# Decay scores in blocks of 32 columns, the mask ahead of a weight split, and 11 extra products ahead of the channel sums, in a two-layer HGRN2 and Mamba-2 kernel

## The reference

```python
bc = jnp.cumsum(logf, axis=2)                 # decay within a chunk
q_dec = q * jnp.exp(bc)
att = jnp.einsum('bnthd,bnshd->bnhts', q_dec, k * jnp.exp(-bc))
att = jnp.where(jnp.tril(jnp.ones((HG_CHUNK, HG_CHUNK), bool)), att, 0.0)
o_intra = jnp.einsum('bnhts,bnshv->bnthv', att, v)
...
x = x + mx[2] * rmsnorm(yx, post_norm[l, 0])
hx = modulate(rmsnorm(x, pre_norm[l, 1]), mx[3], mx[4])
```

## Time and profile before

| | |
|---|---|
| median of 3 runs | 1364.66 us (1364.53 to 1365.32) |
| the profiled execution | 1364.83 us |
| its span in the trace | 1363.1 us |
| PE busy | 1314.1 us, 96% |
| DVE busy | 873.2 us, 64% |
| ACT busy | 657.5 us, 48% |
| head loop and its tail | about 60 to 390 us |
| output projection and sums of layer 0 | about 387 to 422 us |

### The profile page before, as it was taken

The page is one execution under the profiler, slowest core; times in us unless marked ns, Lnnn a source line. Parts: engine busy times, 40 slices in busy tenths (PEclk is TensorE's granted clock), DMA queues, the critical chain, the costliest instruction groups (busy, mean ns, idle before and its releaser), DMA issues. The chain is left out here.

```text
span 1363.1 us, 21145 instructions
## 1 busy us (share of the span) xinstructions
PE 1314.1 (96%) x7954; PEld 1109.6 (81%) x7954; DVE 873.2 (64%) x1718; ACT 657.5 (48%) x1037; POOL 338.4 (25%) x236
## 2 busy tenths in 40 slices
PE   5999999999999999999999999999999999999997
PEld 2678888888775888888888867889888879899997
DVE  4577776767769544322443787877777776775673
ACT  4444444444446533323333357455555654774664
POOL 1000000000202655304553020111111140683771
PEclk9999999999999999999999999999999999999999
DMA  9633433236552443234324342633333348366753
GB/s 345 191 124 126 135 123 122 81 126 199 173 185 62 150 113 87 67 108 124 92 81 134 101 140 67 192 92 91 92 92 91 95 159 255 106 197 176 217 156 108
DMA packets 274790, 183.21 MB, mean 134 GB/s; under 512 B 6642, under 2 KB 249106, under 8 KB 274706
## 3 DMA queue, kind: packets, MB, share of 16 engines
q1 hardware_dynamic: 274162, 180.00, 44.0%
q10 hardware_dynamic: 544, 2.10, 0.4%
HBM read 181.03 MB, written 1.05 MB: 134 GB/s over the span
## 5 line engine op out<-in xcount | busy, mean ns | idle before, releaser
L2180 PE MATMUL bank<-hh,wh 128*128 128x512 f32 (+1 forms) x1298 | 457.0, 352 | 6.4 <-DVE wl L1374 4.4
L2182 PE MATMUL bank<-hh,wl 128*128 128x512 f32 (+1 forms) x1298 | 452.0, 348 | 0.0
L2181 PE MATMUL bank<-hl,wh 128*128 128x512 f32 (+1 forms) x1298 | 451.7, 348 | 0.0
L842 ACT ACTIVATE wh<-wraw 128x1024 fp32r<-128x1024 f32 (+2 forms) x265 | 257.0, 985 | 74.7 <-PE bank L2182 50.7
L2180 PEld LDWEIGHTS bank<-hh,wh 128*128 128x128 f32 x1298 | 244.5, 188 | 41.5 <-DVE wl L1374 6.6
L1374 DVE TENSOR_TENSOR wl<-wraw,wh 128x1024 fp32r<-128x1024 f32 (+2 forms) x171 | 189.3, 1127 | 138.1 <-ACT wh L842 138.0
L2182 PEld LDWEIGHTS bank<-hh,wl 128*128 128x128 f32 x1298 | 244.2, 188 | 32.5
L1835 DVE SCALAR_TENSOR_TENSOR conv<-bank,pv,conv 128x189 f32<-128x189 f32 (+3 forms) x396 | 172.4, 436 | 153.0 <-ACT conv L1113 138.0
L2181 PEld LDWEIGHTS bank<-hl,wh 128*128 128x128 f32 x1298 | 244.4, 188 | 30.2
L730 POOL TENSOR_TENSOR wl<-wraw,wh 128x1024 fp32r<-128x1024 f32 (+2 forms) x87 | 199.1, 2293 | 197.1 <-ACT wh L842 196.7
L776 POOL TENSOR_TENSOR hl<-yT,hh 128x512 fp32r<-128x512 f32 x13 | 19.6, 1535 | 368.8 <-DVE gates L1735 357.9
(11 more groups left out here) (348 smaller groups left out, 2095.6 us busy)
## 6 DMA issues: line engine op xcount, KB each, us to landing
wraw<-in_ffn_w_up SPq DMA_DIRECT2D x88, 512.0 KB, 4.0
araw<-in_ada_w SPq DMA_DIRECT2D x40, 1024.0 KB, 7.5
wraw<-in_mb_w_in SPq DMA_DIRECT2D x48, 512.0 KB, 4.0
wraw<-in_hg_w_in SPq DMA_DIRECT2D x40, 512.0 KB, 3.8
wraw<-in_ffn_w_down SPq DMA_DIRECT2D x32, 512.0 KB, 4.0
wraw<-in_mb_w_out SPq DMA_DIRECT2D x16, 512.0 KB, 4.9
gates<-in_ada_w SPq DMA_DIRECT2D x5, 1024.0 KB, 9.5
wraw<-in_hg_w_out SPq DMA_DIRECT2D x8, 512.0 KB, 4.9
```

The source lines that it names most:

```text
L842: act.activation(slot(whp, n, 0, size), wraw[:, n % SLOTS, 0:size], ACT.Copy).then_inc(w_hi, 1)
L2180: pe.matmul(dst, W, hi(k), start=(k == 0), stop=False, **skip)
L2181: pe.matmul(dst, W, lo(k), start=False, stop=False, **skip)
L2182: ins = pe.matmul(dst, L, hi(k), start=False, stop=(k == nk - 1), **skip)
```

## The change

Four edits. **Scores:** the 4 products of 128 x 128 become 16 of 32 x 32, only the diagonal blocks, going through the four groups of 32 output partitions in turn; the 8 beside the diagonal stay; the 4 of 64 x 64 become 8 of 32 x 64. Blocks that no product writes are now left from what the bank held, and DVE clears bank 6 once at the start. **Semaphore:** `qk_ready` goes up behind L1733, and a new `ke_ready` behind L1734, for which `ke` waits. **DVE:** in each turn `mask_att(p,0)` stands ahead of the split of the first weight piece. **Sums:** behind the last tile of the output projection of layer 0, 11 products go into bank 0 ahead of `both_sums`; they wait until that bank has been read and a weight piece is split.

```diff
@@ DVE, start
+        dve.memset(bank[6][:, :], 0.0)
         params(0)
@@ gate_products
-            V.tensor_tensor(parts(qx2[d]), far(C[:, :], 1 - first), w2(1 - first), ALU.mult)
-            V.tensor_tensor(ch(B), ch(A), s[:, 2, :].unsqueeze(2).to_broadcast([P, NCH, CH]), ALU.mult).then_inc(qk_ready, 1)
+            V.tensor_tensor(parts(qx2[d]), far(C[:, :], 1 - first), w2(1 - first), ALU.mult).then_inc(qk_ready, 1)
+            V.tensor_tensor(ch(B), ch(A), s[:, 2, :].unsqueeze(2).to_broadcast([P, NCH, CH]), ALU.mult).then_inc(ke_ready, 1)
@@ head loop of DVE
+            if S:
+                mask_att(p, 0)
             if h:
                 split_lo(5 * h + 3)
-            if S:
-                mask_att(p, 0)
@@ att(h, d)
-            for t in range(4):
-                r = slice(t * P, (t + 1) * P)
-                pe.matmul(bank[plan.bank(key)][:, r], gA[d][:, r], gC[d][:, r], start=True, stop=True)
+            for c in range(NCH):
+                k, r = c % 4, slice(c * CH, (c + 1) * CH)
+                pe.matmul(bank[plan.bank(key)][k * CH:(k + 1) * CH, r], gA[d][:, r], gC[d][:, r], start=True, stop=True,
+                          skip_group_check=True)
...
-                ins = pe.matmul(bank[plan.bank(key)][2 * CH * d:2 * CH * (d + 1), c:c + 2 * CH], kx2[d][:, t, :], qx2[d][:, t, :],
-                                start=True, stop=True, skip_group_check=True)
+                for j in range(2):
+                    k = 2 * d + j
+                    ins = pe.matmul(bank[plan.bank(key)][k * CH:(k + 1) * CH, c:c + 2 * CH], kx2[d][:, t, j * CH:(j + 1) * CH],
+                                    qx2[d][:, t, :], start=True, stop=True, skip_group_check=True)
@@ ke(h, d)
+            pe.wait_ge(ke_ready, 2 * h + d + 1)
@@ last_tile
+            if (l, s) == (0, 0):
+                plan.wait_emptied(pe, ("y", 0, 4))
+                stay_busy(0, 11, at["up", 0, 0, 0, 0])
```

More of the change, by code:

```diff
@@ L545, in program @@
     d_ready, small_ready, en_ready = sem("d_ready"), sem("small_ready"), sem("en_ready")
-    qk_ready, qin_ready = sem("qk_ready"), sem("qin_ready")
+    qk_ready, ke_ready, qin_ready = sem("qk_ready"), sem("ke_ready"), sem("qin_ready")
     v_ready, ket_ready, att_ready = sem("v_ready"), sem("ket_ready"), sem("att_ready")
```

## The result

The changed kernel takes **1357.03 us** (median of 4 runs, 1356.50 to 1357.08), the kernel before 1364.81 (4 runs, 1364.53 to 1365.32): ratio 0.9942, 95% interval 0.9926 to 0.9958, so 7.8 us less where 9.2 were forecast. The profiled executions took 1357.05 and 1364.83 us. The forecast stood 1.6 us too low, inside its range. By the traces its sum had one term too small (the score blocks, by 2.1 us), one that didn't come (1.7 us of clock), and two losses that it didn't have (1.1 and 0.6 us in layer 1): 9.2 + 2.1 - 1.7 - 1.1 - 0.6 = 7.9.

What follows compares the result with a forecast made beforehand. PE was taken as the bound, busy 1314.1 of 1363.1 us, with a few standstills. Head loop 5.8, clock at 88 us 1.7 and sums 1.7 make 9.2 us less: median 1355.4, range 1353.0 to 1359.2.

Steps and rivals of the forecast that it cites:

- the loop: Head loop: 1.14 us at kv(0,0), 0.50 at att(0,1) and 4.2 over six turns, 5.8 us saved in all.
- The score block: Head loop: 1.38 us from first product to ke instead of 1.97; saves 0.50 us where PE isn't held.
- four groups at once: Score blocks, rival: first 32 records 0.008 us apart, the loop gives 7.8 us, 1353.4 us in all; chance 0.09.
- The rival of PE's feeding: Score blocks: 0.024 us a record, block 1.63 us; time 1357.2, or 1358.9 if the clock falls too; chance 0.14.
- Which savings count: Head loop: att(p,1) waits for DVE's states with 0.11 us to spare, so each turn saves 0.70 us, six turns 4.2.
- the fast value: Head loop: 0.98 us saved per turn if the first 32 score records are 0.008 us apart.
- The tail: End of the head loop: DVE's chain behind f(7,0) sets the time, ke(7,1) waits for the states; nothing saved.
- a rival with 0.06: Sums or tail: the products don't keep the clock, or a new gap ahead of ke(7,1) loses it; 1357.1 us.
- The clock at 88 us: Second turn: the gap ahead of kv(0,0) becomes about 2.0 us and the clock is kept, saving 1.7 us.
- Mask and small edits: Head loop and start: earlier mask brings 1.14 us at kv(0,0), nothing counted in other turns; semaphore and bank clearing nothing.
- The sums: Ahead of layer 0's sums: 11 products fill the 2.57 us gap and keep the clock, saving 1.7 us.
- A shift is kept: Behind the sums: PE is busy in every slice, so the 9.2 us saved until there last to the end.

Runs made afterwards that it cites:

- e5: Changed kernel with its 16 diagonal products ordered one column group after the other instead of one in each group in turn; 1358.49 us, ratio 0.9958 to the kernel before.
- e3: Changed kernel with DVE's masking put back behind the split of the weights; 1359.04 us, ratio 0.9960 to the kernel before.
- e4: Kernel before with only the masking moved ahead of the split of the weights; 1363.05 us beside 1364.68, ratio 0.9988.
- e2: Kernel before with only the 11 products before the sums added; 1364.04 us beside 1364.68, ratio 0.9994.
- e1: Changed kernel without the 11 products before the sums; 1357.90 us, ratio 0.9955 to the kernel before.
- e11: Kernel before with one added wait, GpSimd's fifth subtraction of layer 1's Mamba output behind VectorE's predicated copy; 1363.67 us beside 1364.83, ratio 0.9995.
- e8: Changed kernel with 7 products ahead of kv(0,0) and nine output-projection products moved ahead of ke(7,1); 1356.36 us, ratio 0.9943 to the kernel before.

## Why the prediction was right, and where it wasn't

Part of the hit is luck: the loop gave 2.1 us more than its term, and 3.4 us went missing elsewhere (1.7 of clock at 88 us, 1.1 and 0.6 in layer 1).

**The score block: right in kind, too long.** I took 0.0167 us a record; it is 0.008, the bound for four groups at once (block 1.10 forecast there, 1.07 measured; the 1.13 beside it in the prediction is a slip, since 1.38 - 0.28 = 1.10). My own reading, some 0.03 for a record alone and two groups at once, halved again would have given this value. The order of the groups makes it (e5: 0.022 on average, when products in a row share a group). The rival of PE's feeding is dead. The Trainium skill (TensorE: Matmul & The Clock Gate, section "Wait — 56ns, not 53.3ns?") has starts never closer than about 25 ns. Taken over all groups, the trace disagrees: 32 starts in 0.26 us are a third of that apart. Inside one group the starts, about 0.026 to 0.032 us apart, do keep to it.

**Which savings count: right.** The wait ahead of `att(p,1)` came out at 0.40 us with PE 0.15 behind the states, and a turn gave 0.98, the fast value. With 1.23 at `kv(0,0)` and 0.78 at `att(0,1)` the loop gave 7.9 instead of 5.8.

**The tail: its shift right, its gap missed.** It gave nothing, as forecast. But 1.67 us of what the blocks saved turned into idling ahead of `ke(7,1)`, where I had put "nothing": a gap of 2.2 to 2.4 us behind which the clock fell in 6 of 7 traces, at 1.4 to 1.6 us where the shift shows it. I had this only as part of a rival with 0.06.

**The clock at 88 us: the step that failed as a step.** "I take it as kept, 1.7, by a small margin" treats the outcome as fixed by the gap's length. It isn't: at this place it fell after 2.0 to 2.4 us in 4 traces and stayed in 5, and one program did both. Each kernel has such gaps, the kernel before two (88 us and the sums), the changed one two (88 us and `ke(7,1)`). Where it does fall or stay, it is worth nearly what I said (1.6 for 1.7).

**Mask and small edits: right.** The mask's place gave its 1.1 us at `kv(0,0)` (e3, e4) and nothing in the other turns. The new semaphore and the clearing of bank 6 were not tried apart; no wait in the trace is theirs.

**The sums: right, 1.7** by the trace, twice. But a median gains less, since the kernel before doesn't lose this clock in every execution: 0.6 in e2, and 0.3 to 0.9 by e1. That this is the reason for the difference is argued from the kept clock in e11, not shown. The times on record fit it: the 21 executions of the kernel before beside e2 lie in three groups, 3 at 1362.4 to 1362.9, 11 at 1364.1 to 1364.8 and 7 at 1365.7 to 1366.7 us, as none, one or both losses would have it. The 21 beside e11 cover the same range without such steps.

**"A shift is kept": wrong by 1.7 us, 1.1 of them for a cause in the sum's base.** I subtracted from one execution whose copy at 1099 us took 0.73 us, and the ten others without the wait have 1.84 to 1.85. The median didn't show it: that execution had lost the clock twice, and lay only 0.17 us from the median of three. That the two peculiarities cancelled there is argued. Against the second trace of the kernel before the changed one gains 9.0 us: 7.9 + 1.7, less 0.6. These 0.6 are the wait at 1131 us for the transfer of weights. They are no steady cost of the change: in the second trace of the changed kernel it is 0.3, and traces of the other kernels differ there by up to 0.6 us from the kernel before, in both directions. Why is open.

## What to carry over

The small products of this kernel got cheap because neighbours in the order went to different column groups: the same 32 instructions took 1.07 us in one order and 1.43 in another. When a block on the busiest engine gets shorter, look up the next thing that it waits for, and price the gap twice: in its own length, and in the clock behind it. A gap whose cost varies between executions makes a single trace a poor base for a sum: read two, and either fill such gaps or reorder what they wait for; mending two of them, and a collision of two engines, was worth 4 us here, half as much again as the change.

## What was not expected of the hardware

- The same idle stretch in the same program may cost TensorE's clock or not: 2.09 and 2.23 us, within 0.01, in two traces of the changed kernel, with opposite outcomes at both places. Behind 2.59 us it was kept once, behind 1.99 lost once; of 1.80 and less none in the table lost it. No experiment here varied what may decide between them.
- VectorE's predicated copy and GpSimd's subtraction of 128x512, starting together, cost 1.1 us on the copy (1.85 for 0.73) or 0.6 on GpSimd's side (4.97 for 4.36 over three), and the copy lost in 10 of the 11 traces that have no wait between them. The order of the starts didn't decide it: in e8 GpSimd's start was recorded 1 ns ahead and in the changed kernel VectorE's, and the copy took 1.84 and 1.85 us.
- 32-column products in four column groups start 0.008 us apart on average (0.007 inside a round of four, one round every 0.032), and their records of the next kind (L2320, L2326) overlap with them.
